# Where the masked matrices of the next level are made in a blocked triangular inverse

## What is computed

```python
c = GDN_CHUNK                                   # 64
a_mat = jnp.where(strict, jnp.einsum('bhncd,bhnsd->bhncs', k_beta, k) * decay, 0.0)
t_inv = lax.linalg.triangular_solve(a_mat + eye, jnp.broadcast_to(eye, a_mat.shape),
                                    left_side=True, lower=True, unit_diagonal=True)
u = jnp.einsum('bhncs,bhnse->bhnce', t_inv, v_beta)
w = jnp.einsum('bhncs,bhnsd->bhncd', t_inv, k_beta * jnp.exp(g)[..., None])
```

## Time and profile before

| quantity | value |
|---|---|
| median of three runs | 1889.95 us |
| the profiled execution's own time | 1888.03 us |
| its span in the trace | 1885.9 us |
| mean granted clock of TensorE in it | 0.951 of full speed |
| the five levels of the inverse | about 221.7 to 305.4 us of the span |

### The profile page before, as it was taken

How to read it: one execution, slowest core, us unless ns; L and a number is a source line. 1 busy time by engine, 2 the same in 40 slices (tenths; PEclk the granted TensorE clock), 3 DMA queues, 4 the chain that set the end, 5 groups by cost and what they waited for, 6 DMA issues and landing times. The chain is left out here.

```text
span 1885.9 us, 28850 instructions
## 1 busy us (share of the span) xinstructions
PE 1706.8 (91%) x9877; PEld 1555.0 (82%) x9877; DVE 1407.3 (75%) x2542; ACT 690.9 (37%) x1048; POOL 478.0 (25%) x340
## 2 busy tenths in 40 slices
PE   6997778886979999998969998997799999999997
PEld 3875576544758899998869998997799999999996
DVE  4777766877332388798899998975688788788786
ACT  4763222235142233423324443432333333333333
POOL 1000000000110367776713332344122222222220
PEclk8998998897989999998979999999899999999999
DMA  3221000000223358876858887899799999999993
GB/s 109 96 96 38 1 1 35 23 1 24 66 78 101 135 164 270 280 241 222 288 164 318 327 322 257 323 378 379 272 331 355 345 343 359 331 360 339 344 357 109
DMA packets 149135, 404.54 MB, mean 215 GB/s; under 512 B 14100, under 2 KB 71700, under 8 KB 145592
## 3 DMA queue, kind: packets, MB, share of 16 engines
q1 hardware_dynamic: 108728, 243.99, 38.8%
q0 software_dynamic: 36864, 134.23, 18.8%
q10 hardware_dynamic: 3456, 25.17, 3.3%
HBM read 350.90 MB, written 52.44 MB: 214 GB/s over the span
## 5 line engine op out<-in xcount | busy, mean ns | idle before, releaser
L1579 PE MATMUL bank<-h_hi,rt_u_hi 128*128 128x384 f32 x1024 | 356.5, 348 | 34.3 <-DVE rt_u_lo L1369 24.8
L1711 PE MATMUL bank<-va_w_hi,va_v_hi 128*128 128x384 f32 x1024 | 343.4, 335 | 16.2 <-DVE va_w_lo L1676 16.2
L1581 PE MATMUL bank<-h_hi,rt_u_lo 128*128 128x384 f32 x1024 | 347.0, 339 | 0.0
L1580 PE MATMUL bank<-h_lo,rt_u_hi 128*128 128x384 f32 x1024 | 346.9, 339 | 0.0
L1713 PE MATMUL bank<-va_w_hi,va_v_lo 128*128 128x384 f32 x1024 | 343.2, 335 | 0.0
L1712 PE MATMUL bank<-va_w_lo,va_v_hi 128*128 128x384 f32 x1024 | 343.1, 335 | 0.0
L1297 ACT ACTIVATE rt_u_hi<-raw 128x1024 fp32r<-128x1024 f32 x128 | 135.6, 1060 | 410.8 <-PE bank L1581 343.8
L1662 ACT ACTIVATE va_v_hi<-raw 128x1024 fp32r<-128x1024 f32 x128 | 135.7, 1060 | 345.3 <-PE bank L1713 341.2
L1340 POOL DMA_INDIRECT h<-u_rows_dram,own_experts x128 | 169.0, 1320 | 280.5 <-DVE rt_waste L1376 270.1
L1787 POOL DMA_INDIRECT qy<-v_dram,own_experts x128 | 130.7, 1021 | 409.5 <-DVE va_own L1696 403.5
L1676 DVE TENSOR_TENSOR va_v_lo<-raw,va_v_hi 128x1024 fp32r<-128x1024 f32 x128 | 156.8, 1225 | 103.2 <-ACT va_v_hi L1662 98.3
(11 more groups left out here) (323 smaller groups left out, 2703.2 us busy)
## 6 DMA issues: line engine op xcount, KB each, us to landing
raw<-u_dram SPq DMA_DIRECT2D x128, 512.0 KB
raw<-v_dram SPq DMA_DIRECT2D x128, 512.0 KB
active_scratch<-rt_act SPq DMA_DIRECT2D x128, 192.0 KB
gates_scratch<-early ACTq DMA_DIRECT2D x24, 1024.0 KB, 7.1
early<-gates_scratch SPq DMA_DIRECT2D x16, 1536.0 KB
early<-active_scratch SPq DMA_DIRECT2D x128, 192.0 KB
in_raw<-w_in_dram SPq DMA_DIRECT2D x22, 512.0 KB, 3.5
query_raw<-w_query_dram SPq DMA_DIRECT2D x16, 512.0 KB, 3.5
```

The costliest lines, as they stand in the source:

```text
L1579: mm(bank, u_hi[:, j % 2, cols], hi[:, c, 0:TD], start=c == 0, stop=False)
L1580: mm(bank, u_hi[:, j % 2, cols], lo[:, c, 0:TD], start=False, stop=False)
L1581: last = mm(bank, u_lo[:, j % 2, cols], hi[:, c, 0:TD], start=False, stop=c == DC - 1)
L1711: mm(bank, v_hi[:, j, cols], w_hi[:, j, :], start=start, stop=False)
```

## The change

The body of the mask loop becomes the function `level_mask(level, h)`, with the same wait and the same instruction. The masks of level 1 are made in front of the loop over the levels. In each level, VectorE then first makes the four masks of the next level (each after this level's product x of its head has read the buffer) and only then does this level's subtractions. In level 5 there are no masks any more. The number of instructions, their sizes and the waits of all other engines stay as they are.

```diff
                 dve.wait_ge(s["strip_out"], 16)
+                def level_mask(level, h):
+                    if level > 1:
+                        dve.wait_ge(s["x"], H * (level - 2) + h + 1)
+                    tt_(blocks(mt_u[:, h, :]), blocks(at[:, h, :]), t.per_block(C_MT + level),
+                        ALU.mult).then_inc(s["mt"], 1)
+
+                for h in range(H):
+                    level_mask(1, h)
                 for level in range(1, LEVELS):
-                    for h in range(H):
-                        if level > 1:
-                            dve.wait_ge(s["x"], H * (level - 2) + h + 1)
-                        tt_(blocks(mt_u[:, h, :]), blocks(at[:, h, :]), t.per_block(C_MT + level),
-                            ALU.mult).then_inc(s["mt"], 1)
+                    if level + 1 < LEVELS:
+                        for h in range(H):
+                            level_mask(level + 1, h)
                     for h in range(H):
                         dve.wait_ge(s["tx"], H * (level - 1) + h + 1)
                         if level < LEVELS - 1:
```

## The result

The changed kernel took 1870.63 us (median of four runs, 1867.26 to 1873.57) against 1889.54 us (four runs, 1887.15 to 1893.63): a ratio of 0.9897, 95% interval 0.9871 to 0.9923, or 18.9 us less. Its profiled execution took 1868.87 us; the one before 1888.03.

The account below looks back on a forecast made before the run. TensorE's product x was taken to wait on VectorE's masks once per level. Gaps of 13.67 us plus 2.71 and 2.0 for the clock, less 0.4 or so, gave 17.95 off 1889.95: 1872.0 us, range 1867.4 to 1879.

Parts of the forecast that it names:

- The gaps: TensorE's idle times before x in levels 2 to 5 go: 1.94, 2.07, 4.93 and 4.73, together 13.67 us.
- The clock: TensorE's granted clock stays full in levels 4 and 5, making x there 2.71 and 2.0 us shorter.
- The rival of a low clock: Clock stays low in levels 4 and 5: 3.8 us given back, gain 14.1, 1875.8 us; chance 0.18.
- VectorE in level 4: VectorE becomes the later engine: masks end at 273.00, subtractions 0.9 us late, TensorE waits 0.55 us.
- 0.4 or so: Microseconds taken off the gain because TensorE's tx is held up in level 4.
- The sum: First subtraction of level 5 comes at 282.75 instead of 300.70, a gain of 17.95 us.
- Does it reach the end?: Recurrence, output projection and later stages start when the mixer's work is done, so the gain counts in full.
- the recurrence and what follows take longer than before: One of the named signs of being wrong, to be looked for in the changed kernel's profile; no size given.
- given back behind the inverse: Only 4.0 us from levels 2 and 3 reach the end, for instance through a lower recurrence clock: 1886 us; chance 0.10.
- The blocked queue: Waiting masks block VectorE's first-in-first-out queue, at worst 2.50 us in four levels, 10.0 us: 1900 us; chance 0.02.

Follow-up runs that it names:

- r4: The kernel before, with five 128x512 matmuls into an unused bank in front of x in levels 4 and 5: 1890.91 us, ratio 1.0008.
- r5: The changed kernel with every mask of levels 2 to 5 made twice, one after the other: 1876.8 us, ratio 0.994 to the kernel before.
- r7: The changed kernel with all twenty masks on GpSimd, none on VectorE: 1872.7 us, ratio 0.9907 to the kernel before.
- r11: The changed kernel with masks of levels 2 to 5 on GpSimd and the recurrence's wide up-projections put between narrow output matmuls: 1863.09 us.
- r3: The changed kernel with only the masks of levels 4 and 5 early, those of levels 2 and 3 where they were: 1874.77 us, ratio 0.9925.
- r2: The changed kernel with only the masks of levels 2 and 3 early, those of levels 4 and 5 where they were: 1878.34 us, ratio 0.9938.
- r10: The same program as r2, run once more: 1878.77 us, ratio 0.9934 to the kernel before.

## Why the prediction was right

The forecast was 1872.0 us, 1867.4 to 1879; measured 1870.63.

**The gaps.** All four went, and level 1's 3.49 us stayed, as said. x began at 239.56, 254.94, 265.88 and 277.70; the working had 239.77, about 255.2, 266.32 and 277.85. The small lead comes from the changed trace starting 0.12 us sooner, and from adding up idle times only: where x follows without a break, it starts a little before the last matmul of the work ahead has ended.

**The clock.** 1.00 in levels 4 and 5, x in 3.86 us. That the long gaps bring the low clock is shown by r4. The rival of a low clock did not come in any of the three traces of the changed kernel: its levels took 60.1, 60.1 and 59.9 us.

**VectorE in level 4.** The late subtraction (272.63; worked out 273.00), TensorE's wait (0.74 us; worked out 0.55) and the idle time before level 5 (1.25 us; worked out 1.0) are all in the trace. That VectorE is the bound there is shown by r5, and by r7 and r11, which have no masks on VectorE in this level. They also show that the working sized this term too small: the lateness costs 11.82 - 10.84 = 1.0 us, not "0.4 or so".

**The sum.** 17.95 us to the first subtraction of level 5, measured 18.14, of which 0.12 lies ahead of the levels. That it fits to 0.1 us is luck in part: the 0.6 us too little for the lateness was made up by the small leads of x named under the gaps, which the working did not count (0.6 us, what is left of 18.0 - 13.7 - 4.7 + 1.0).

**Does it reach the end?** This step held for the size and not for its reasoning, and so by luck. I found "nothing tied to absolute time" behind the levels; but what follows them does not take the same time in each trace. The recurrence took 1.9 to 4.3 us more in the three traces of the changed kernel (95.3, 93.1, 92.9) than in the two of before (91.0, 91.1); from the last step to the last output it was 3.3 us less on the mean (1470.7, 1472.8 and 1471.4 against 1475.9 and 1474.0). The two nearly cancel: from the first step to the last output it is 1566.0, 1565.9 and 1564.3 us against 1567.0 and 1565.0. I had named as a sign of being wrong that "the recurrence and what follows take longer than before": it came for the recurrence alone, and not for the two together. In the recurrence the granted clock makes the difference, 14.9 us at 0.54 against 10.7 at 1.00 between two steps of one kernel; whether the inverse's new timing decides where it falls is not shown, and what shortens the part behind stays open. The rival "given back behind the inverse" named a lower clock in the recurrence, which came, but not its price of 14 us.

**The blocked queue** had a chance of 0.02. The queue does block for a moment: 0.74 us in level 4. r5 shows that even twice the masks do not turn it: that kernel is still 11.7 us faster than the kernel before.

**The parts.** The change is worth about 18 us in the levels: 13.7 us of gaps, 4.7 of clock, 0.6 of the small leads, less 1.0 for VectorE's lateness. That split, taken from the trace of before, holds for that trace only. r3 shows that the short gaps can cost the clock as well (2.9 us), and r2 with r10 that the long ones need not cost as much.

## What to carry to other kernels

Where an engine that is idle in one part of a loop holds up the bound engine in the next part, move what depends only on old data into the idle part, ahead of the waits, and check with the rows that it ends before the first result that it now stands in front of. A gap on TensorE costs more than itself when the granted clock falls behind it, but a gain of clock in one stage need not reach the end (r4): price a clock effect over the whole kernel and not in the stage alone, and trace more than one execution before giving a few microseconds to an edit. Before moving work to GpSimd, look for VectorE instructions with two inputs in SBUF beside it.

## What was not expected of the hardware

The clock's pattern depends on more than the gap in front of a stretch. Behind the same gap of 4.93 us, x took 6.67 and 6.71 us in the kernel before and 5.56 and 5.38 in r2 and r10; behind 1.94 us it took 3.96 or 5.47. Nor is it a matter of the kernel alone. The two traces of the kernel before agree with each other up to the end of the recurrence; those of the changed kernel part at one stretch of it (0.54 against 1.00), and r2 and r10, one program, took 87.5 and 93.1 us for the recurrence. So in a single pair of traces 4 to 6 us of difference can lie in a stage that the change does not touch. A VectorE instruction with two inputs in SBUF took 1.64 us beside one of GpSimd instead of 0.69.
